# Making all low halves of the weights on VectorE from the thirteenth weight step on

## The reference

```python
u = rms_norm(h, ln) @ w_in
...
return h + (o * jax.nn.silu(gate)) @ w_o
```

## Time and profile before

| | |
|---|---|
| times of three runs | 1490.26, 1491.66, 1491.86 us |
| profiled execution: span, first to last instruction | 1489.8 us |
| PE busy | 1456.9 us, 98% |
| DVE busy | 635.0 us, 43% |
| ACT busy | 686.8 us, 46% |
| GpSimd busy | 708.4 us, 48% |
| mean granted TensorE clock | 0.992 |
| low halves on GpSimd, 128x1024 | 224, mean 2496 ns |
| low halves on DVE, 128x1024 | 225, mean 1359 ns |
| DMA | 248.50 MB, mean 167 GB/s |

### The profile page before, as it was taken

How to read it: one execution, slowest core, us unless ns; L and a number is a source line. 1 busy time by engine, 2 the same in 40 slices (tenths; PEclk the granted TensorE clock), 3 DMA queues, 4 the chain that set the end, 5 groups by cost and what they waited for, 6 DMA issues and landing times.

```text
span 1489.8 us, 22557 instructions
## 1 busy us (share of the span) xinstructions
PE 1456.9 (98%) x8018; PEld 1260.5 (85%) x8018; DVE 635.0 (43%) x1024; ACT 686.8 (46%) x975; POOL 708.4 (48%) x332
## 2 busy tenths in 40 slices
PE   6999999999999999999999999999999999999998
PEld 4888888899988888888888888888887888888998
DVE  7455566544953234333334333433342333333332
ACT  4354555544334445444544544444544544444442
POOL 3443444433545444644553554564465355445432
PEclk9899999999999999999999999999999999999999
DMA  6443334335545554654554554555455455455444
GB/s 235 156 148 131 130 123 141 134 128 184 169 167 187 190 175 145 191 190 150 180 191 157 170 189 151 170 187 179 147 187 190 151 179 191 150 177 192 162 156 142
DMA packets 69344, 248.50 MB, mean 167 GB/s; under 512 B 7696, under 2 KB 8080, under 8 KB 69136
## 3 DMA queue, kind: packets, MB, share of 16 engines
q1 hardware_dynamic: 69120, 246.28, 48.7%
q10 hardware_dynamic: 144, 1.05, 0.2%
HBM read 245.20 MB, written 2.10 MB: 166 GB/s over the span
## 4 chain that ended last, share of the span: by engine, by line
PE 38%; issue 31%; POOL 26%; DVE 4%; POOLq 0%; DMA 0%; ACT 0%; SPq 0%; ACTq 0%; DVEq 0%
PE acc L1069 35%; POOL w_lo L378 21%; POOL root L392 2%; DVE xa_lo L712 1%; POOL phase L438 1%; POOL rms L389 1%; PE turn L1099 1%; PE pv_bank L1111 1%; PE score L1289 1%; DVE w_lo L698 1%; DVE prob L743 0%; DVE xb_hi L709 0%; POOL rms L396 0%; DVE xa_hi L709 0%; DVE res L980 0%
## 5 line engine op out<-in xcount | busy, mean ns | idle before, releaser
L378 POOL TENSOR_TENSOR w_lo<-raw,w_hi 128x1024 fp32r<-128x1024 f32 x232 | 574.1, 2475 | 636.5 <-ACT w_hi L462 636.3
L462 ACT ACTIVATE w_hi<-raw 128x1024 fp32r<-128x1024 f32 (+1 forms) x465 | 485.4, 1050 | 342.8 <-PE acc L1069 331.8
L698 DVE TENSOR_TENSOR w_lo<-raw,w_hi 128x1024 fp32r<-128x1024 f32 (+1 forms) x233 | 313.2, 1345 | 439.7 <-ACT w_hi L462 439.7
L1069 PE MATMUL acc<-w_hi,xa_hi 128*128 128x512 f32 (+1 forms) x1088 | 407.0, 374 | 10.7 <-DVE w_lo L698 10.7
L1069 PE MATMUL acc<-w_hi,xa_lo 128*128 128x512 f32 (+1 forms) x1088 | 399.0, 367 | 0.0
L1069 PE MATMUL acc<-w_lo,xa_hi 128*128 128x512 f32 (+1 forms) x1088 | 398.2, 366 | 0.0
L1069 PE MATMUL acc<-w_hi,xb_hi 128*128 128x512 f32 (+1 forms) x640 | 252.6, 395 | 4.3 <-POOL w_lo L378 2.4
L1069 PE MATMUL acc<-w_hi,xb_lo 128*128 128x512 f32 (+1 forms) x640 | 247.4, 387 | 0.0
L1069 PE MATMUL acc<-w_lo,xb_hi 128*128 128x512 f32 (+1 forms) x640 | 247.3, 386 | 0.0
L1069 PEld LDWEIGHTS acc<-w_hi,xa_hi 128*128 128x128 f32 x1088 | 206.6, 190 | 44.5 <-issue 13.4
L1069 PEld LDWEIGHTS acc<-w_hi,xa_lo 128*128 128x128 f32 x1088 | 206.2, 190 | 33.8
(11 more groups left out here) (116 smaller groups left out, 1076.1 us busy)
## 6 DMA issues: line engine op xcount, KB each, us to landing
raw<-in_w_b SPq DMA_DIRECT2D x320, 512.0 KB, 3.3
raw<-in_w_gate SPq DMA_DIRECT2D x32, 512.0 KB, 3.2
raw<-in_w_out_a SPq DMA_DIRECT2D x32, 512.0 KB, 3.3
raw<-in_w_out_b SPq DMA_DIRECT2D x32, 512.0 KB, 3.3
raw<-in_w_in SPq DMA_DIRECT2D x16, 512.0 KB, 4.3
raw<-in_w_kv SPq DMA_DIRECT2D x16, 512.0 KB, 3.3
raw<-in_w_q SPq DMA_DIRECT2D x16, 384.0 KB, 3.0
res<-in_xT SPq DMA_DIRECT2D x4, 512.0 KB, 7.3
```

What stands on the lines that cost most here:

```text
L378: nc.gpsimd.tensor_tensor(w[1][:, s, 0:width], raw[:, s, 0:width], w[0][:, s, 0:width].bitcast(F32), ALU.subtract).then_inc(lo_ready[1], 1)
L462: nc.scalar.activation(w[0][:, s, 0:width], raw[:, s, 0:width], ACT.Copy).then_inc(hi_ready, 1)
L698: nc.vector.tensor_tensor(w[1][:, s, 0:width], raw[:, s, 0:width], w[0][:, s, 0:width].bitcast(F32), ALU.subtract).then_inc(lo_ready[0], 1)
L1069: last = nc.tensor.matmul(out, x(a), y(b), start=start and k == 0, stop=stop and k == 2, **more)
```

## The change

Low halves of steps 0 to 12 stay as they are. From step 13 (`LOW_0`) on every low half is made by DVE and counted in `lo_ready[0]` alone. GpSimd's calls of `lows` from there on are gone. `low_of` tells SP and PE which counter and which count stands for a step. On DVE no call of `lows` had to be added where the loops already called it for every step with a guard for the odd ones; in layer B, where odd steps were called only in GpSimd's list, one call is added at the start of each quarter. (Blank lines at the head of the file go as well, so line numbers after the change are about 15 to 25 lower.)

```diff
+LOW_0 = 13
...
-        def half_count(n, static_n):
+        def low_of(n, static_n):
-            return n // 2 + 1 if isinstance(n, int) else n[0] * (n[1] // 2) + (static_n // 2 + 1)
+            if static_n < LOW_0:
+                return lo_ready[static_n % 2], static_n // 2 + 1
+            return lo_ready[0], step_count(n, static_n) - (LOW_0 // 2 - 1)
...   (SP, load)
-                    if isinstance(n, int):
-                        sp.wait_ge(lo_ready[n % 2], (n - RING) // 2 + 1)
-                    else:
-                        i, per = n
-                        sp.wait_ge(lo_ready[static_n % 2], i * (per // 2) + ((static_n - RING) // 2 + 1))
+                    signal, count = low_of(n - RING if isinstance(n, int) else n, static_n - RING)
+                    sp.wait_ge(signal, count)
...   (GpSimd)
-                lows(n + 4, n + 4)
+                if n + 4 < LOW_0 and n % 2:
+                    lows(n + 4, n + 4)
...
-                    lows((i, MLA_STEPS), MLA_0 + 4 + s, Q_STEP if s in (2, 3) else STEP)
-            for k in range(OUT_STEPS):
-                lows(OUT_A_0 + 4 + k, OUT_A_0 + 4 + k)
...
-                    lows((i, B_STEPS), B_0 + 4 + 2 * s)
...
-            for k in range(OUT_STEPS - 4):
-                lows(OUT_B_0 + 4 + k, OUT_B_0 + 4 + k)
...   (VectorE)
-                if static_n % 2:
+                if static_n < LOW_0 and static_n % 2:
                     return
...
             def b_pair(i, par, attend):
                 for s in range(B_QUARTERS):
+                    lows((i, B_STEPS), B_0 + 4 + 2 * s)
...   (PE, use_step)
-                pe.wait_ge(lo_ready[static_n % 2], half_count(n, static_n))
+                signal, count = low_of(n, static_n)
+                pe.wait_ge(signal, count)
```

More of the change, by code:

```diff
@@ L372, in lows @@
             def lows(n, static_n, width=STEP):
-                if static_n % 2 == 0:
-                    return
                 s = static_n % RING
```

## The result

The changed kernel takes 1482.27 us (median of 4 runs, 1481.64 to 1482.71) beside 1490.96 us for the kernel before (4 runs, 1489.89 to 1491.86): the ratio is 0.9945, 95% interval [0.9931, 0.9959]. That is 8.7 us; 6.1 us were predicted, and 1485.6 us against 1482.3. The measured time lies between the case that was forecast (1483 to 1488 us) and rival 4 (1481), inside the stated range. In the profiled executions the span went from 1489.8 to 1480.3 us.

The account below looks back on a forecast made before the run. PE, busy nearly throughout, was taken as the bound, through its waits and the clock lost behind them. Gains of 14.9 us less losses of 8.8 gave -6.1: 1491.7 becomes 1485.6 us; 8 in 10 within 1481 to 1493.

Parts of the forecast that it names:

- the case that was forecast: Whole kernel: gains at PE's waits outweigh the losses from added low halves, 1483 to 1488 us; chance 0.56.
- rival 4: Layer B: losses are 0.5 or less, since DVE gets to the scaling first; 1481 us, chance 0.09.
- Gains (gate, output projection of A, start of B): Three large PE waits and the half clock behind them go or nearly go: 3.4, 3.5 and 5.2 us gained.
- Key rows and `og` in A: Layer A: waits for key rows go, 2.8 us gained; added low half delays `og` seven times by 0.2, 1.4 us lost.
- Second latent: Layer A, once: added low half between sums and scaling holds GpSimd's power, making PE about 0.9 us late.
- Pair to pair in B: Second low half ahead of the scaling makes PE late, 0.95 us at each of five places; bounds 0.75 and 1.0.
- After pair 7: Layer B, behind the last pair, where steps are longer: a loss of 0.65 us.
- The page's rule: DVE and GpSimd share ports, first starter holds them; by it L396 finishes first and the sum is about 1.2 us better.
- Loop turns: Layer B, pairs 3 to 4 and 5 to 6: added low half makes PE 0.55 us late each.
- 1 (cancel): Gains and losses cancel through one more tight hand-over or 1.7 us lost per pair in B; 1491 us, chance 0.24.
- 2 (clock falls at the pair changes): Layer B: idle of 1 us drops the clock at eight places, 15 us more; 1500.5 us, chance 0.08.
- 3 (long by themselves): Long DVE operations are not due to GpSimd, so no gains, only added low halves; about 1502 us, chance 0.03.

Follow-up runs that it names:

- Experiment 1: Changed kernel plus unused two-operand subtractions on GpSimd at the old places of its odd low halves, in A and early B: 1498.64 us.
- 2: Changed kernel, but DVE makes all low halves only from step 13 to 112; from step 113 every second one is GpSimd's: 1483.11 us.
- 3: Split of the kernel before kept up to step 112, all low halves on DVE from step 113 (layer B) on: 1493.05 us.
- 5: Changed kernel, but DVE makes all low halves only from step 13 to 124; then every second one is GpSimd's: 1477.55 us.
- 7: Changed kernel, with layer A's low half asked for after step 7 moved behind the next pair's piece of attention: 1478.99 us.
- 8: Changed kernel with the edit of 7, B's added low halves moved behind the scaling at pair changes, and step 19's behind the second latent's scaling: 1472.22 us.

## Why the prediction was right, and where its sizes were off

- **Gains (gate, output projection of A, start of B).** Right in mechanism, place and size: 3.3, 3.6 and 4.9 us for 3.4, 3.5 and 5.2. Experiment 1 takes them back with GpSimd's work alone (the gate's in part), 2, 3 and 5 place the last one. Of the 5.2, 0.2 were counted twice: the window from 429 begins 0.36 us before PE does. The method that worked was to add the clock behind a wait (window length times 1 minus the granted clock) to the wait itself.
- **Key rows and `og` in A.** Predicted 2.8 - 1.4 = 1.4 us, measured 2.0. The waits for key rows went (2.8 us), those for `og` grew by 1.1. The push of 0.2 us on the row at 251.42 is there. In the kernel before, PE begins its step at 250.25 and that row comes 1.17 us later; after, PE begins at 246.10 and it comes 1.33 us later, behind the added low half:

```profile
250.25 0.48 PE L1069 MATMUL acc<-w_hi,xb_hi 128*128 128x512 f32 x1
```

```profile
246.10 0.48 PE L1048 MATMUL acc<-w_hi,xb_hi 128*128 128x512 f32 x1
246.29 1.23 DVE L675 TENSOR_TENSOR w_lo<-raw,w_hi 128x1024 fp32r<-128x1024 f32 x1 [0.38 <-ACT w_hi L439]
247.43 0.28 DVE L708 TENSOR_TENSOR oT_lo<-og_bank,oT_hi 128x128 f32 x1
```

That is 0.16 us, and the wait went from 0.38 to 0.53. What the walk left out is a larger part of the same wait, shown by 7: the low half after step 7 lengthens GpSimd's power by 0.93 us. That was so before the change too (253.43, 1.94 us), so it cost little new, but 3 us could be had there.
- **Second latent.** 0.9 predicted, 0.9 measured, gone when the low half moves (8).
- **Pair to pair in B: the term that was mis-sized.** 0.95 us were taken, near the upper bound by which L396 waits through both low halves. It doesn't: it ends 1.28 us into the pair of low halves (1010.90 to 1012.21), just as beside a single one, and the five plain places cost 0.74 to 0.84, near the lower bound of 0.75. After pair 7: 0.5 for 0.65. The one long case that argued for the upper bound, 4.78 us from 396.07, is a wide operation; the small one was through after one low half. The difference is 1.0 us with the place after pair 7.
- **The page's rule.** The Trainium skill (SBUF — State Buffer, section "SBUF: two separate sides") has the shared pair of ports as an exclusive lock that goes to whoever starts first. On the exclusion this case agrees (experiment 1). The prediction read the earlier trace rows as speaking against "first"; the rows don't carry that. In every trace here the multiplication L396 (L378 after) starts at most 0.03 us before the low half that holds it, and ends some 0.05 us behind it; at 1010.90 a gate scaling is still under way on VectorE (1010.40 to 1011.01). With the same lead of 0.02 us `halve` at 601.45 was the one that held the low half. What decides is open. The sum by the rule was said to be 1.2 us better (1.0 by the lower bound of 5.5); the losses came out at that size, by another way, since the multiplication was held and the scaling came no later for it.
- **Loop turns: not foreseen.** Each was put at a loss of 0.55. The delays of the scaling are there (0.47 and 0.46 us of idle), but PE's own idle at the turn shrank by 1.06 and 0.83 us. Two executions of the same code give +0.6 and -0.2 us for both turns, so this is 0.9 to 1.7 us better than predicted, and no run shows why.
- **Sum.** The span came out 3.4 us lower than forecast: 1.7 from the turns, 1.0 pair to pair with the last one, 0.6 in the pairs of A, 0.3 before step 17, less 0.3 at the start of B and some tenths of rounding. All small, nearly all one way. The 1.0 is a loss taken from the upper half of its bounds. The 1.7 and 0.3 are not a merit of the reasoning: up to 1.1 of them is chance of the execution profiled (the second one of the same code gains 8.4 us, not 9.5), and the rest of the turns has no known cause. By the medians the change gave 8.7 us for 6.1, 2.6 more than forecast.
- **Rivals.** 1 (cancel) needed one more hand-over with little to spare; PE's list of waits has none. 2 (clock falls at the pair changes): idle of 0.25 to 0.64 us, clock 1.00. 3 (long by themselves): `xb_hi` takes 1.23 us after, and 1 makes such pieces long again. 4 (losses of 0.5 or less, 1481) came nearest in time, by another way: the losses stood at 0.8, the turns paid.

## What to carry to other kernels

When a helper engine's work moves to the engine that feeds the bottleneck, price the long two-operand pieces of both that overlap, not the sum of busy time: here that overlap and the half clock behind it cost 12 us in three places. Then look at the order on the receiving engine: a piece that is due three steps later must not stand in front of a short chain that the bottleneck waits for, nor beside the helper's small link of that chain. Low halves moved behind such a chain, at four kinds of places, brought 13 us, more than the change did.

## What the runs showed of the hardware

- Small GpSimd instructions are held too, beyond their own length: the power of 128x4 takes 1.01 us alone and 1.94 us beside a low half; the multiplication of 128x4 0.26 us with no low half beside it (1019.26 in experiment 3) and 1.31 beside one.
- Of two low halves back to back a small GpSimd instruction waits for one, not for both. A wide one (128x512) that began at 412.59 in experiment 1 took 4.36 us instead of 1.04, beside three low halves in a row that took their usual 3.5 us together. It can go the other way too: `halve` (3.60 us) got in between two low halves, and the second took 4.66 us.
- A wait costs PE more than the idle time that the profile gives: the six at B's changes of pair outside the turns sum to 3.3 us (0.25 to 0.64 each) and cost 4.4 us of progress. The matmul ahead of an idle is shown with its pipeline (0.39 us, where the next starts 0.23 us later). In layer A moving one low half (7) removed an idle of 0.53 us per pair for `og` and brought back 0.39 us for key rows; the pair got 0.41 us shorter all the same (29.94 to 29.53).
- Idle times of PE of 1.39 to 1.57 us left the granted clock at 1.00 in five places (loop turns of before, 2 and 5; 1.53 and 1.40 us in 1), as did 1.72 us at 23.85 in 8; 1.81, 1.93, 2.06 and 2.15 us were followed by windows of 5 to 8 us with 0.57 to 0.79. So a wait that is only cut can give back its clock: in 1 the gate's wait is 0.4 us shorter than before the change and the stage 1.5 us, where the prediction had said that a cut wait still costs the clock.
